# Matmuls without a reader in front of eleven waits of TensorE

## The chip, the cores and the metric

The kernel runs on one core of one Trainium2 chip. The metric is the device time of one execution in microseconds; each kernel is run several times and the median is given. TensorE, which does the matrix products, runs at one of two clock levels, 1.2 or 2.4 GHz. The trace shows which one it was granted, as a share of the full clock: 0.50 or 1.00.

## The reference

One call computes two blocks of two layers each, on 512 tokens of width 1024. The first block also carries 256 context tokens, the second one 16 meta tokens. Cut to what matters:

```python
for l in range(2):                                   # first block
    h  = modulate(rmsnorm(x, g_norm1[l]), sh1, sc1)
    hc = modulate(rmsnorm(xc, g_norm1[l]), sh1c, sc1c)
    pf, mq, mk, mv, mo, mg, cq, ckv, kr = split_proj(h @ w_in[l])   # and the same of hc
    y_f = fourier_mix(pf)
    y_m = mlstm_output(hf, hb, mo, g_mlstm[l])       # chunkwise scans in both directions
    y_a = merge_heads(blocked_attend(qn, qr, (lat_keys, ctx_keys)))
    x = x + ga1 * (jnp.concatenate([y_f, y_m, y_a], axis=-1) @ w_out[l])
    x = x + ga2 * sqrelu_mlp(modulate(rmsnorm(x, g_norm2[l]), sh2, sc2), w_up[l], w_down[l])
    ...                                              # the context likewise where l is 0
for i in range(2):                                   # second block
    h = hybrid_layer(h, attn_norm[i], w_in[i], ...)  # rmsnorm, fox attention, retention, gated MLP
out = rmsnorm_2(h, final_norm)[:, N_META:]
```

An rmsnorm needs the sum of the squares of all 1024 features of a token before the first feature can be scaled. Those sums stand at the edges between the stages.

## The kernel before

Activations lie with the features on the 128 partitions (8 tiles of 128 features, `KT`) and the tokens along the free dimension: 768 (`ALL`), 512 (`LAT`) or 528 (`SEQ2`). Weights come from memory in blocks of 128x1024. Each block is split into a high and a low part of reduced precision (`hi_ring` by ScalarE, L260; `lo_ring` by VectorE, L270), activations too (`h_hi`, `h_lo`), and each product is made three times: high by high, low by high, high by low (`tile_product`, L343). `product_pair` works on two weight blocks at once, the second three feature tiles behind the first (`LAG`), since it follows the operand tiles as they are made.

What the change touches:

- `Norm.on_pe` (line 677 on): the first norm of a layer. A product of `ones` and the sums of squares (`sumsq`, added up by GpSimd in L658) spreads the total over all partitions (`product`, L332). ScalarE takes the root (L690), VectorE inverts it (L706) and makes the operand tiles (L723, L716). In the first layer of the first block the squares are `presummed` in the stage before.
- `LateNorm.on_pe` (line 925 on): the norm in front of the first block's MLP, whose products start before the factor is known.
- the Fourier stage (line 1147 on), whose first product takes the tiles of `Norm`.
- the end of the mLSTM scans (line 2045 on): after the last chunk the outputs are normed and gated by the other engines, and TensorE turns them (transposes, L2050).
- `square_columns` in the mixing stage of the second block (line 2464 on): the sums of squares as columns (L2470 to L2477), and the products behind the first pair of weight blocks (line 2629 on), which wait until VectorE has taken a result out of PSUM (L2980).

Of the kernel before, what the change touches and what calls it, by code (L numbers as in the profile page):

```python
# [31 lines left out]
ALL = LAT + CTX  # L32
# [104 lines left out]
class Core:  # L137
# [68 lines left out]
    def buf(self, j):  # L206

        j %= BUFS
        return self.ps[:, 2 * j:2 * j + 2, :].rearrange("p b n -> p (b n)")

    def width(self, g):
        return NARROW if any(a <= g < b for a, b in self.narrow) else BLOCK
# [452 lines left out]
class Norm:  # L665
# [11 lines left out]
    def on_pe(self, pe):  # L677
        core = self.core
        if self.presummed:
            return  # L680
        pe.wait_ge(core.added.sem, core.added.at(0))
        product(core.nc, self.acc, [core.ones[:]], [core.sumsq[:]], self.tokens, P).then_inc(self.summed.sem, 1)

# [202 lines left out]
class LateNorm:  # L886
# [37 lines left out]

    def on_pe(self, pe):
        core = self.core
        pe.wait_ge(core.added.sem, core.added.at(0))
        product(core.nc, self.acc, [core.ones[:]], [core.sumsq[:]], self.tokens, P).then_inc(self.summed.sem, 1)

# [184 lines left out]
def fourier(core, arena, acts, mix, tokens, norm, l, mod_first, mods):  # L1114

    nc, dram = core.nc, core.dram
    tiles_of = [(0, LT, 0, LAT)] + ([(LT, TT, LAT, ALL)] if tokens == ALL else [])
    a = Alloc(arena, KT * ALL)
    u, spec = a(2, ALL), a(TT, 4 * P)
    half = [LAT // 2 + 1, CTX // 2 + 1] if not mods else [LAT, CTX]  # L1120
    at = [0, half[0]]
    cos = [a(LT, half[0]), a(CT, half[1])]
    sin = [a(LT, half[0]), a(CT, half[1])]

    mod = Modulation(core, l, mod_first, mods, a(MOD_RING, BLOCK).rearrange("p r n -> p (r n)"),
                     silu_rows(mix))
    norm.tmp = a(2, ALL)
    odd = u[:, :, 0:ALL]
    odd_in = core.counter("fourier_odd_copied")
    tables = core.counter("tables_in")  # L1130
    evacuated = core.counter("fourier_evacuated")
    feature = core.counter("fourier_features")
    token = core.counter("fourier_tokens")
    nt = tokens // P
    with nc.Block(no_gpsimd_drain=True) as block:
        @block.sync
        def _(sp):
            core.feed(sp, FOURIER_BLOCKS)
            if mods:
                mod.feed(sp)  # L1140

        @block.gpsimd
        def _(pool):
            for name, dst in (("cos_lat", cos[0]), ("sin_lat", sin[0]), ("cos_ctx", cos[1]), ("sin_ctx", sin[1])):
                pool.dma_start(dst, dram[name][:, :, 0:dst.shape[2]]).then_inc(tables.sem, 16)

        @block.tensor
        def _(pe):
            norm.on_pe(pe)

            product_pair(core, pe, 0, 0, UNROLL, KT, acts, tokens,
                         lambda j: pe.wait_ge(core.free.sem, core.free.at(j + 1)), norm.wait_tile(pe))
            pe.wait_ge(core.free.sem, core.free.at(BUFS + FOURIER_BLOCKS))
            for t in range(nt):
                if t >= 2:
                    pe.wait_ge(evacuated.sem, evacuated.at(t - 1))
                for j in range(2):
                    last = nc.tensor.matmul(core.ps[:, 4 + t % 2, j * 2 * P:(j + 1) * 2 * P],
                                            u[:, j, t * P:(t + 1) * P], core.const[:, C_DFT:C_END],
                                            start=True, stop=True)  # L1160
                last.then_inc(feature.sem, 1)
            pe.wait_ge(evacuated.sem, evacuated.at(nt))
            pe.wait_ge(tables.sem, tables.at(64))
            for j in range(2):
                for n, (t0, t1, c0, c1) in enumerate(tiles_of):
                    if mods:
                        for t in range(t0, t1):
                            for part, table in enumerate((cos[n], sin[n])):
                                last = nc.tensor.matmul(core.buf(j)[:, c0:c1],
                                                        spec[:, t, (2 * j + part) * P:(2 * j + part + 1) * P],  # L1170
                                                        table[:, t - t0, :], start=t == t0 and part == 0,
                                                        stop=t == t1 - 1 and part == 1)
                        continue
                    for part, table in enumerate((cos[n], sin[n])):
                        for t in range(t0, t1):
                            last = nc.tensor.matmul(core.ps[:, 2 * j + part, at[n]:at[n] + half[n]],
                                                    spec[:, t, (2 * j + part) * P:(2 * j + part + 1) * P],
                                                    table[:, t - t0, :], start=t == t0, stop=t == t1 - 1)
                last.then_inc(token.sem, 1)

        @block.scalar
        def _(act):
            mod.load_rows(act)
            norm.on_act(act)
            if mods:
                mod.sigmoid(act)
            for j in range(FOURIER_BLOCKS):
                core.part_hi(act, 0, j + SPLIT)
                core.computed(act, 0, j)
                nc.scalar.activation(u[:, j, 0:tokens], core.buf(j)[:, 0:tokens], ACT.Copy).then_inc(core.free.sem, 1)  # L1190
            if not mods:
                mod.sigmoid(act)
            for j in range(2):
                act.wait_ge(token.sem, token.at(j + 1))
                if mods:
                    nc.scalar.activation(mix[:, j, 0:tokens], core.buf(j)[:, 0:tokens], ACT.Copy)
                    continue
                n = at[len(tiles_of) - 1] + half[len(tiles_of) - 1]
                nc.scalar.activation(odd[:, j, 0:n], core.ps[:, 2 * j + 1, 0:n], ACT.Copy).then_inc(odd_in.sem, 1)

        @block.vector
        def _(dve):
            norm.on_dve(dve, norm.tmp)
            if mods:
                mod.begin(dve)
            for j in range(FOURIER_BLOCKS):
                core.part_lo(dve, 0, j + SPLIT)
            for t in range(nt):
                dve.wait_ge(feature.sem, feature.at(t + 1))
                nc.vector.tensor_copy(spec[:, t, :], core.ps[:, 4 + t % 2, :]).then_inc(evacuated.sem, 1)  # L1210
            if not mods:
                mod.begin(dve)
            if mods:
                mod.all_sums(dve)
                mod.finish(dve)
            for j in range(0 if mods else 2):
                dve.wait_ge(odd_in.sem, odd_in.at(j + 1))
                for n, (t0, t1, c0, c1) in enumerate(tiles_of):
                    h, e, o = half[n], core.ps[:, 2 * j, at[n]:at[n] + half[n]], odd[:, j, at[n]:at[n] + half[n]]
                    nc.vector.tensor_tensor(mix[:, j, c0:c0 + h], e, o, ALU.add)  # L1220
                    nc.vector.tensor_tensor(mix[:, j, c0 + h:c1][:, ::-1], e[:, 1:h - 1], o[:, 1:h - 1], ALU.subtract)
    core.close(FOURIER_BLOCKS, FOURIER_BLOCKS)
    mod.close()
    norm.close()
    tables.close(64)
    evacuated.close(nt)
    feature.close(nt)
    token.close(2)
    odd_in.close(0 if mods else 2)
# [662 lines left out]
def mlstm(core, arena, scratch, masks, pick, m, mix, ctx_out):  # L1892
# [8 lines left out]
    out = a(TT, hid)  # L1901
# [45 lines left out]
    with nc.Block(no_gpsimd_drain=True) as block:  # L1947
# [31 lines left out]
        def _(pe):  # L1979
# [57 lines left out]
            for u in range(len(steps_all)):  # L2037
                n = n_out(u)
                if u in outs and n + 1 < len(outs):
                    weigh(outs[n + 1])  # L2040
                if u in outs:
                    sums(u)
                if u in upds:
                    grow(u)
            for n, t in enumerate(tiles_done):
                pe.wait_ge(normed.sem, normed.at(n + 1))
                if n >= 4:
# [225 lines left out]
NORM_AT = 4  # L2273
# [12 lines left out]
def hybrid_layer(core, h, l):  # L2286
# [5 lines left out]
    entry, last = l == 0, l == DEPTH - 1  # L2292
# [133 lines left out]
    with nc.Block(no_gpsimd_drain=True) as block:  # L2426
# [34 lines left out]
        def _(pe):  # L2461
            free = lambda j: pe.wait_ge(core.free.sem, core.free.at(j + 1))

            def square_columns():

                pe.wait_ge(core.added.sem, core.added.at(0))
                if entry:
                    pe.wait_ge(gain_added.sem, gain_added.at(0))
                for t, (c, n) in enumerate(TOKEN_TILES[0:LT] if entry else TOKEN_TILES):
                    ins = nc.tensor.matmul(core.ps[0:n, NORM_AT, t:t + 1], core.sumsq[:, c:c + n], core.ones[:, 0:1],  # L2470
                                           start=True, stop=True)
                if entry:
                    for t in range(LT):
# [4 lines left out]
                                           start=True, stop=True)  # L2478
# [148 lines left out]
                    factor_rows()  # L2627
            ins.then_inc(core.done, 1)
            pe.wait_ge(ones_in.sem, ones_in.at(1))
            for j in range(2, MIX_BLOCKS):  # L2630
                w = core.arrived(pe, 0, j)
                free(j)
# [863 lines left out]
```

## Time and profile before

| | |
|---|---|
| median of three runs | 3328.93 us (3321.52, 3328.93, 3332.76) |
| profiled execution, first to last instruction (span) | 3326.5 us |
| TensorE, matmuls busy | 3110.3 us (94%), 19072 records |
| TensorE, weight loads busy | 2726.2 us (82%) |
| VectorE busy | 1787.3 us (54%) |
| ScalarE busy | 1176.6 us (35%) |
| GpSimd busy | 299.1 us (9%) |
| mean granted TensorE clock | 0.966 |

The profiled execution has no time of its own beside its span; the median of the runs lies 2.4 us above the span. Busy shares are over the whole span. Matmuls overlap in the pipeline, so the busy time of TensorE does not tell how fast it works; the granted clock does.

### The profile page before, as it was taken

To read this page: it belongs to the slowest core of one execution; us is meant where nothing else is said; L and a number is where in the kernel's file an instruction comes from. 1 tells how busy PE (TensorE), PEld (TensorE's weight loads), DVE (VectorE), ACT (ScalarE), POOL (GpSimd) and SP (SyncE) were. 2 spreads that over 40 slices of the span, in tenths; PEclk is the share of its full clock that TensorE was granted. 3 is DMA by queue.
4 is the path that set the end of the run, shared out by engine and by line. 5 is a ranking of instruction groups with operands and counts; after the bars stand their busy time and mean duration, and the time that the engine had idled before them with its cause. 6 is when DMAs were issued, how large, how long until landed. Compare 5 with 4: busy or idle time off the path is not lost. (4 is left out here: it accounts for less than half of the span.)

```text
span 3326.5 us, 49141 instructions
## 1 busy us (share of the span) xinstructions
PE 3110.3 (94%) x19072; PEld 2726.2 (82%) x19072; DVE 1787.3 (54%) x2840; ACT 1176.6 (35%) x1843; POOL 299.1 (9%) x268
## 2 busy tenths in 40 slices
PE   3999889999997999899999999999999999899998
PEld 2678877888886687789987897899999898778886
DVE  8558677465565567554443545554344345554444
ACT  3243534232232443544444332343223332243222
POOL 1000210101102001112223000010001000010001
PEclk8999889999998998899999999999999999999999
DMA  7231033232332231122222111122323211122322
GB/s 265 74 111 60 12 114 121 95 126 101 107 116 95 68 116 45 46 84 93 93 90 89 57 46 45 52 89 83 107 84 101 71 45 51 51 93 84 107 88 95
DMA packets 105693, 288.68 MB, mean 87 GB/s; under 512 B 36272, under 2 KB 36400, under 8 KB 104272
## 3 DMA queue, kind: packets, MB, share of 16 engines
q1 hardware_dynamic: 100304, 269.73, 24.3%
q0 software_dynamic: 3808, 10.38, 0.9%
q10 hardware_dynamic: 1440, 6.62, 0.5%
q8 instruction: 97, 1.59, 0.2%
q14 instruction: 44, 0.36, 0.0%
HBM read 284.56 MB, written 2.10 MB: 86 GB/s over the span
## 5 line engine op out<-in xcount | busy, mean ns | idle before, releaser
L343 PE MATMUL ps<-h_hi,hi_ring 128*128 128x512 f32 (+2 forms) x2672 | 872.3, 326 | 64.5 <-DVE h_lo L716 41.3
L270 DVE TENSOR_TENSOR lo_ring<-ring,hi_ring 128x1024 fp32r<-128x1024 f32 (+1 forms) x410 | 484.6, 1182 | 700.9 <-ACT hi_ring L260 696.6
L343 PE MATMUL ps<-h_lo,hi_ring 128*128 128x512 f32 (+2 forms) x2672 | 843.5, 316 | 0.0
L343 PE MATMUL ps<-h_hi,lo_ring 128*128 128x512 f32 (+2 forms) x2672 | 840.5, 315 | 0.0
L260 ACT ACTIVATE hi_ring<-ring 128x1024 fp32r<-128x1024 f32 (+1 forms) x410 | 420.1, 1025 | 1032.2 <-PE ps L343 992.0
L343 PEld LDWEIGHTS ps<-h_hi,hi_ring 128*128 128x128 f32 x2672 | 513.9, 192 | 126.5 <-issue 81.8
L343 PEld LDWEIGHTS ps<-h_lo,hi_ring 128*128 128x128 f32 x2672 | 515.1, 193 | 33.6 <-issue 3.9
L343 PEld LDWEIGHTS ps<-h_hi,lo_ring 128*128 128x128 f32 x2672 | 512.5, 192 | 30.9
L343 PE MATMUL ps<-ffn_operand,hi_ring 128*128 128x264 f32 (+1 forms) x2112 | 479.7, 322 | 1.5 <-DVE lo_ring L270 1.5
L343 PEld LDWEIGHTS ps<-ffn_operand,hi_ring 128*128 128x128 f32 x2112 | 350.5, 188 | 35.1 <-issue 1.8
L343 PE MATMUL ps<-ffn_operand,lo_ring 128*128 128x264 f32 (+1 forms) x1056 | 339.1, 321 | 0.0
L343 PE MATMUL ps<-hid_hi,hi_ring 128*128 128x512 f32 (+1 forms) x768 | 275.4, 359 | 3.3 <-DVE hid_lo L1087 3.3
L343 PE MATMUL ps<-hid_lo,hi_ring 128*128 128x512 f32 (+1 forms) x768 | 274.8, 358 | 0.0
L343 PE MATMUL ps<-hid_hi,lo_ring 128*128 128x512 f32 (+1 forms) x768 | 274.7, 358 | 0.0
L343 PE MATMUL ps<-hidden,hi_ring 128*128 128x264 f32 (+1 forms) x1056 | 239.4, 321 | 0.0
L343 PEld LDWEIGHTS ps<-ffn_operand,lo_ring 128*128 128x128 f32 x1056 | 198.4, 188 | 16.2
L343 PEld LDWEIGHTS ps<-hidden,hi_ring 128*128 128x128 f32 x1056 | 175.2, 188 | 16.3
L343 PE MATMUL ps<-hidden,lo_ring 128*128 128x264 f32 (+1 forms) x528 | 169.5, 321 | 0.0
L343 PEld LDWEIGHTS ps<-hid_hi,hi_ring 128*128 128x128 f32 x768 | 144.8, 189 | 28.4 <-DVE hid_lo L1087 5.1
L343 PEld LDWEIGHTS ps<-hid_hi,lo_ring 128*128 128x128 f32 x768 | 144.8, 189 | 23.1
L343 PEld LDWEIGHTS ps<-hid_lo,hi_ring 128*128 128x128 f32 x768 | 144.7, 188 | 22.8
L453 DVE SCALAR_TENSOR_TENSOR silu_rows<-mod_ring,silu_rows 128x1024 f32<-128x1024 f32 x128 | 150.1, 1218 | 1.2 <-DMA mod_ring<-w_mod_dram 1.2
(360 smaller groups left out, 3842.6 us busy)
## 6 DMA issues: line engine op xcount, KB each, us to landing
ring<-weights_dram SPq DMA_DIRECT2D x334, 512.0 KB, 3.3
mod_ring<-w_mod_dram SPq DMA_DIRECT2D x64, 512.0 KB, 4.2
ring<-weights_dram SPq DMA_DIRECT2D x76, 384.0 KB, 3.0
arena<-w_mod_dram SPq DMA_DIRECT2D x48, 512.0 KB, 3.4
x<-x_dram SPq DMA_DIRECT2D x1, 3072.0 KB, 16.6
arena<-c_rows_dram ACTq DMA_DIRECT2D x3, 1024.0 KB, 6.6
arena<-ret_decay_dram POOLq DMA_DIRECT2D x2, 1056.0 KB, 6.0
silu_rows<-c_rows_dram ACTq DMA_DIRECT2D x2, 1024.0 KB, 5.3
```

The source lines that it names most:

```text
L260: self.nc.scalar.activation(self.hi_ring[:, g % SPLIT, 0:w], self.ring[:, g % RING, 0:w], ACT.Copy).then_inc(self.hi, 1)
L270: self.nc.vector.tensor_tensor(self.lo_ring[:, g % SPLIT, 0:w], self.ring[:, g % RING, 0:w], self.hi_ring[:, g % SPLIT, 0:w], ALU.subtract ...
L343: ins = nc.tensor.matmul(out[0:m, c:c + n], w, a[:, t0:t0 + n], start=first and k == 0 and p == 0, stop=last and k == kts - 1 and p == 2)
L453: core.nc.vector.scalar_tensor_tensor(self.scratch[:, c, :], self.ring[:, g % MOD_RING, :], 1.0, self.rows[:, c, :], ALU.mult, ALU.mult, a ...
```

## The change

`Core.unread(n)` issues n matmuls of `ones` by `ones`, 128x128 in f32, into a corner of PSUM that nobody reads. They are called at the places named above, each time just ahead of a wait, with counts of 18 to 38.

```diff
--- before.py
+++ after.py
@@ -208,6 +208,13 @@
         j %= BUFS
         return self.ps[:, 2 * j:2 * j + 2, :].rearrange("p b n -> p (b n)")
 
+    def unread(self, n, out=None):
+
+        out = self.ps[:, 7, 384:512] if out is None else out
+        for _ in range(n):
+            self.nc.tensor.matmul(out, self.ones[:], self.ones[:, 0:out.shape[1]], start=True, stop=True,
+                                  skip_group_check=True)
+
     def width(self, g):
         return NARROW if any(a <= g < b for a, b in self.narrow) else BLOCK
 
@@ -678,6 +685,7 @@
         core = self.core
         if self.presummed:
             return
+        core.unread(24)
         pe.wait_ge(core.added.sem, core.added.at(0))
         product(core.nc, self.acc, [core.ones[:]], [core.sumsq[:]], self.tokens, P).then_inc(self.summed.sem, 1)
 
@@ -924,6 +932,7 @@
 
     def on_pe(self, pe):
         core = self.core
+        core.unread(24 if self.tokens == ALL else 19)
         pe.wait_ge(core.added.sem, core.added.at(0))
         product(core.nc, self.acc, [core.ones[:]], [core.sumsq[:]], self.tokens, P).then_inc(self.summed.sem, 1)
 
@@ -1147,6 +1156,11 @@
         @block.tensor
         def _(pe):
             norm.on_pe(pe)
+            if norm.presummed:
+                pe.wait_ge(norm.root.sem, norm.root.at(1))
+                core.unread(22)
+            else:
+                core.unread(38)
 
             product_pair(core, pe, 0, 0, UNROLL, KT, acts, tokens,
                          lambda j: pe.wait_ge(core.free.sem, core.free.at(j + 1)), norm.wait_tile(pe))
@@ -2042,6 +2056,7 @@
                     sums(u)
                 if u in upds:
                     grow(u)
+            core.unread(29, core.ps[:, 3, 384:512])
             for n, t in enumerate(tiles_done):
                 pe.wait_ge(normed.sem, normed.at(n + 1))
                 if n >= 4:
@@ -2463,6 +2478,7 @@
 
             def square_columns():
 
+                core.unread(26 if entry else 19)
                 pe.wait_ge(core.added.sem, core.added.at(0))
                 if entry:
                     pe.wait_ge(gain_added.sem, gain_added.at(0))
@@ -2627,6 +2643,7 @@
                     factor_rows()
             ins.then_inc(core.done, 1)
             pe.wait_ge(ones_in.sem, ones_in.at(1))
+            core.unread(18, core.ps[:, NORM_AT, 384:512])
             for j in range(2, MIX_BLOCKS):
                 w = core.arrived(pe, 0, j)
                 free(j)
```

The places in the order of the program. TensorE at the edge between the first layer's output projection and its MLP; `squares_added` is GpSimd's semaphore for the sums. Before:

```order
1638 L343 MATMUL ps<-h_hi,lo_ring 128x256
1639 L810 UNCONDITIONAL_BRANCH
1640 L1030 UNCONDITIONAL_BRANCH [waits barrier_Pool_Activation_PE_DVE_SP_release]
1641 L332 MATMUL ps<-sumsq,ones 128x512 [waits squares_added]
1642 L332 MATMUL ps<-sumsq,ones 128x256
```

The same place with the change (its lines stand 7 to 9 lower in the file):

```order
1641 L350 MATMUL ps<-h_hi,lo_ring 128x256
1642 L818 UNCONDITIONAL_BRANCH
1643 L1039 UNCONDITIONAL_BRANCH [waits barrier_Pool_Activation_PE_DVE_SP_release]
1644 L215 MATMUL ps<-ones 128x128 x24
1645 L339 MATMUL ps<-sumsq,ones 128x512 [waits squares_added]
1646 L339 MATMUL ps<-sumsq,ones 128x256
```

The 24 matmuls stand between the wait for the barrier and the product that waits for the sums; at four more edges it looks the same with other counts. TensorE behind the first pair of weight blocks of the mixing stage, where `psum_free` is VectorE's semaphore for a free buffer and `fox_ones_in` one for a constant row; with the change:

```order
4266 L350 MATMUL ps<-h_hi,lo_ring 128x264
4267 L215 MATMUL ps<-ones 128x128 [waits fox_ones_in]
4268 L215 MATMUL ps<-ones 128x128 x17
4269 L350 MATMUL ps<-h_hi,hi_ring 128x264 [waits psum_free,block_lo]
4270 L350 MATMUL ps<-h_lo,hi_ring 128x264
```

Here no barrier is in between: the 18 follow the last product of the pair, and the wait for the constant row has moved from the next product to them.

## Rows read from the trace of the kernel before

**Rows 1.** The page, 40 slices of the span: granted clock in tenths

```profile
PEclk8999889999998998899999999999999999999999
```

**Rows 2.** Who TensorE waited for: us in total, times, longest us

```profile
PE ps L343 <- DVE h_lo L716: 41.3, 6, 28.9
PE ps L332 <- POOL sumsq L658: 22.0, 4, 6.3
...
PE ps L343 <- DVE arena L2980: 9.5, 2, 4.8
...
PE ps L343 <- DVE h_lo L857: 5.6, 2, 3.2
```

**Rows 3.** Windows: stretch, length, TensorE busy (records), clock, DMA share, GB/s

```profile
505.42:508.40 2.98, 2.98 (x5) 0.50 0.98 403
1057.05:1059.98 2.93, 2.93 (x4) 0.50 0.95 377
1425.56:1430.00 4.44, 4.44 (x14) 0.50 0.83 229
1803.10:1812.30 9.20, 9.20 (x43) 0.50 0.73 270
...
sum 25.24, PE 25.23; mean PE 5.05
```

**Rows 4.** Windows behind other long waits

```profile
63.55:68.10 4.55, 4.55 (x13) 0.51 1.01 403
428.81:433.30 4.49, 4.49 (x14) 0.50 0.99 413
1373.28:1378.80 5.52, 5.52 (x13) 0.50 0.51 180
1834.47:1839.60 5.13, 5.13 (x23) 0.50 0.28 99
2602.63:2607.60 4.97, 4.97 (x23) 0.50 0.52 176
2607.60:2612.57 4.97, 4.97 (x43) 1.00 0.07 26
1069.57:1081.80 12.23, 10.42 (x22) 0.50 0.00 0
```

**Rows 5.** Barrier events of TensorE: duration ns, first and last start us

```profile
L810 PEldq EVENT_SEMAPHORE  x2: 51/51/51, 499.3 to 503.7; - x2
...
L1007 PEldq EVENT_SEMAPHORE  x2: 51/51/51, 1050.8 to 1055.4; - x2
...
L810 PEldq EVENT_SEMAPHORE  x2: 51/51/51, 1420.5 to 1424.4; - x2
...
L1007 PEldq EVENT_SEMAPHORE  x2: 51/51/51, 1796.6 to 1801.2; - x2
...
L2426 PEldq EVENT_SEMAPHORE  x2: 51/51/51, 2569.8 to 2573.7; - x2
```

**Rows 6.** Timeline at two edges: start us, us, what, [idle before <-releaser]

```profile
503.56 1.80 POOL L658 TENSOR_TENSOR sumsq<-sumsq,arena 128x768 f32<-128x768 f32 x1 [6.52 <-ACT arena L640]
...
505.42 2.93 PE L332 MATMUL ps<-sumsq,ones 128*128 128x512 f32 x4 [6.28 <-POOL sumsq L658]
...
2574.61 2.02 PE L2470 MATMUL ps<-ones,sumsq 128*128 128x1 f32 x10 [4.92 <-POOL sumsq L658]
```

**Rows 7.** Timeline of TensorE: transposes at the slow and at the full clock

```profile
420.99 0.90 PE L2050 MATMUL ps<-const,scratch 128*128 128x128 f32 x3 [7.55 <-ACT scratch L2121]
...
172.67 0.87 PE L1380 MATMUL ps<-const,arena 128*128 128x128 f32 x6 [0.79 <-ACT arena L1460]
```

**Rows 8.** Timeline around the first products of both Fourier stages

```profile
54.93 4.95 DVE L706 RECIPROCAL sumsq<-sumsq 128x768 f32<-128x768 f32 x1 [3.20 <-ACT sumsq L690]
...
1069.57 0.77 PE L343 MATMUL ps<-h_hi,hi_ring 128*128 128x512 f32 x1 [9.59 <-DVE h_lo L716]
...
1071.72 0.80 PE L343 MATMUL ps<-h_hi,hi_ring 128*128 128x512 f32 x1 [0.53 <-DVE h_lo L716]
```

## The prediction

> **What bounds the kernel now.** I read the slices of the page first: TensorE's granted clock is 8 to 9 tenths in most slices, not full [rows 1]. So some of its work runs at 1.2 GHz instead of 2.4 GHz. Next I read the list of waits, to see where the long pauses are: TensorE waits for `h_lo` of the norms, for GpSimd's last addition of squares, and for `arena L2980` [rows 2]. Then the windows from the end of each such wait to the point where the clock is back: the five in [rows 3] are 25.24 us together, all of them with TensorE busy and the clock at 0.50, and [rows 4] has six more (the fifth window there is what the same work looks like once the clock is back). Everything outside is product after product, so TensorE sets the end and a delay of it at a stage edge is carried to the last instruction.
>
> The price of a slow microsecond: 4.97 us at 0.50 hold 23 products, the next 4.97 us at 1.00 hold 43 [rows 4]. So of work that now runs slowly, a share of 1-23/43 = 0.47 would be saved. When the clock comes back: after a restart it takes 3.0 us (505.42 to 508.40), 4.4 (1425.56 to 1430.00) [rows 3], 4.6, 4.5, 5.1 and 5.0 (63.55, 428.81, 1834.47, 2602.63) [rows 4]. I take 4.5 us; the ends are 3.0 and 5.5 (1373.28 to 1378.80).
>
> **The change, part by part.** It removes and moves nothing. It adds 266 matmuls of 128x128 in f32 at eleven places, with no result that anyone reads. Their price has two bounds. Two f32 products in the code are four records in the trace (x4 at 505.42, [rows 6]), so one unread matmul is two records. A 128x128 record costs 0.21 us at the slow clock (three of `L2050` in 0.90 us, of which I count some 0.27 for the emptying of the pipeline) and 0.11 us at the fast one (six of `L1380` in 0.87 us, less some 0.2 of the same) [rows 7]. So an unread matmul costs 0.43 us cold and 0.22 us warm.
>
> *Five stage edges (24, 24, 19, 26, 19).* The waits there are 6.28 us before 505.42 and 4.92 us before 2574.61 [rows 6], and 24 warm unread matmuls are 5.3 us, so they seem to fit. But they stand behind the block's barrier, not at the start of the wait: the order shows the barrier's release on TensorE's queue, then the unread matmuls. The trace dates that release: TensorE's second event at the barrier is at 503.7, 1055.4, 1424.4, 1801.2 and 2573.7 [rows 5]. The actual wait ends at 505.42, 1057.05, 1425.56, 1803.10 [rows 3] and 2574.61 [rows 6]. So only 1.7, 1.6, 1.1, 1.9 and 0.9 us are left to hide in, 7.2 in all (7.0 with 0.05 us at each for the first instruction), because GpSimd's last addition starts at 503.56 and takes 1.80 us [rows 6], and the barrier opens just behind its start. And the clock has fallen by then: TensorE has been idle for four to five microseconds since the last product. So they start cold: 4.5 us until the clock is back hold 4.5/0.43 = 10.5 of them, the rest cost 0.22 each. 24 take 4.5+13.5x0.22 = 7.5 us, 19 take 6.4, 26 take 7.9; together 7.5+7.5+6.4+7.9+6.4 = 35.7. Less the 7.0 that is hidden: the next real product starts 28.7 us later in sum. Queued behind them is the product of the squares, for which ScalarE's root waits, and all products of the stage. What is given back: the 25.24 us of cold work run warm, 0.47x25.24 = 11.9 us. Net +16.8 us. Bounds: with 3.0 us until the clock is back the five take 31.8 us, so +12.9; with 5.5 us +19.3.
>
> At the fourth edge `h_lo` tiles come from ScalarE and VectorE behind the same column sums, so warm TensorE will catch up with them; I take 0.6 us back from the gain there (an estimate between 0 and the 1.5 us of one pair of products).
>
> *After the first pair of the mixing stages (18 and 18).* No barrier is in front: the order puts them right behind the pair, and the semaphore they wait for (`fox_ones_in`) was raised early. The clock is full when they start. They take 18x0.22 = 4.0 us in a wait of 4.75 us (9.5 us for two, [rows 2]). So they cost nothing and the clock should hold. 5.13+4.97 us of cold work [rows 4] become warm: -4.7 us. If the clock fell in the last 0.7 us anyway, this term would be 0.
>
> *At the end of the mLSTM scan (29 and 29).* The wait for the first tile is 7.55 us [rows 7], there is no barrier before it, but the clock is already down when it starts. 4.5+18.5x0.22 = 8.6 us: 1.0 us too late for the first transposes. The transposes themselves get shorter (6x3 at half the price, paced by ScalarE's copies of about half a microsecond), I count -0.5 us for both places, bounds +1 and -1.5. After them a barrier and the splitting of the mix leave TensorE idle again (3.24 us at the first place, [rows 2]), perhaps long enough for the clock to fall again: after 4.75 us it had, at 1834.47 [rows 2, 4]. So of the 4.49+5.52 us of cold work behind [rows 4], worth 4.7 us, I count half: -2.4 us, bounds 0 and -4.7.
>
> Here the Trainium skill has a rule that speaks against this part ("TensorE: Matmul & The Clock Gate", Part 4: PE-mode transpose): transposes do not engage the full clock. The six records of `L1380` are transposes and run at 0.11 us each [rows 7], at the full clock, so the trace does not bear it out for a stretch between other products. By the rule my 0.5 us for the shorter transposes would be gone and the sum half a microsecond longer.
>
> *First Fourier stage (22, behind the root) and the second one (38, behind the squares).* The root is in at 54.93 [rows 8]; the wait ends at 63.55. 4.5+11.5x0.22 = 7.0 us in 8.6 us: hidden. The 38 take 8.4 us in 9.59 us [rows 8]: hidden. But neither gains: the first tiles of `h_lo` come 2.15 us apart (1069.57 and 1071.72, [rows 8]), and TensorE, cold as it is, waits for 1.81 of the 12.23 us [rows 4]. Made faster, it only waits more, and being idle half the time it may lose the clock again when the pairs begin. I count +0.3 us for both, bounds -0.6 and +1.3.
>
> The sum, against the profiled execution: 28.7-11.9+0.6-4.7-0.5-2.4+0.3 = +10.1 us on a span of 3326.5 us, 3336.6 us. The median of the runs shown, 3328.93, lies 2.4 us above that span, so the forecast is 3339.0 us.
>
> **The rivals.**
> *Fitting covers (faster).* If the unread matmuls began when the wait begins (499.14, which is 505.42 less the 6.28 us of [rows 6]), all would be hidden and each cold restart warm: 0.47x(25.24+5.13+4.97+4.49+5.52) = 21.3 us, with the transposes 21.8 us: 3307 us. For it: the counts are about 0.85 of each wait at 0.22 us. Against it: the barrier's release in [rows 5] and the order. It decides at one place: whether the first unread matmul runs before 503.7.
> *Even (no change).* The clock comes back after 3.0 us, as at 505.42, and holds after the scans: late 31.8-7.0 = 24.8, less 11.9, 4.7 and 4.7+0.5, is +3 us: 3332 us. For it: one row of six. Against it: the other five.
> *The unread work doesn't raise the clock.* Then each costs 0.43 us: 48.2-7.0 = 41.2 at the edges, 9.8 at the scans (12.5 against 7.55, twice), 6.7 at the 38, 6.0 at the two 18s, 0.9 at the first: about +65 us, 3394 us. Against it: f32 products of the same kind precede the rise at 505.42 [rows 6].
>
> **How the numbers follow.** The forecast has 0.6, the even case 0.22, the fitting covers 0.08, no rise 0.04; the other 0.06 is for small gains of mechanisms that I don't see. A measurement tells about 0.3% (10 us) from no change, and the forecast of +10.1 lies on that edge: a little over half of it counts as slower, since three of the six restarts of a plain product took 4.6 us or more. That is 0.33, with the 0.04 of no rise and 0.1 of the even case, where the runs fall high by chance: slower 0.47. Same is the rest of the forecast and of the even case and 0.02 of the small gains, 0.41. Faster is 0.08 and the other 0.04 of these, 0.12. The forecast's own range is 3332 to 3346 us; the stated one is 3328 to 3348, leaving out the fitting covers and the case of no rise.
>
> **What would show it.** The unread matmuls start at about 503.8, never at 499.2, and in records 0.21 us apart at first; the product of squares starts some 6 us behind GpSimd's end at the five edges, with TensorE never idle there; the clock's windows behind it read 1.00. At the mixing stages the product after the 4.75 us wait starts at full clock. The second Fourier stage has the same length as before from `h_lo` on. I am wrong if an edge from barrier to product is under 4 us, if the clock falls in the 0.7 us left behind the 18s, or if the time stays under 3329 us.

## The result, and the profile after

The changed kernel takes 3342.11 us in the median (3339.42 to 3345.95, six runs) against 3330.76 us before (3321.52 to 3334.40, six runs). The ratio is 1.0037 with a 95% interval of 1.0024 to 1.0049: slower by 11.4 us, which is small but clear of no change. The forecast was 3339.0 us. In the page of the profiled execution TensorE's clock is up and so is the time:

```profile
span 3340.9 us, 50205 instructions
...
PE 3166.2 (95%) x19604; PEld 2784.5 (83%) x19604; DVE 1788.0 (54%) x2840; ACT 1177.1 (35%) x1843; POOL 299.1 (9%) x268
...
PEclk8999899999999998999999999999999999899999
```

The 532 additional records are the 266 unread matmuls, two each. The mean granted clock rose from 0.966 to 0.975. So the change did what it says, and the kernel still lost: a busier TensorE and a fuller clock are not a shorter path.

TensorE's two events at each barrier, to be compared with [rows 5] (duration ns, first and last start us):

```profile
L818 PEldq EVENT_SEMAPHORE  x2: 51/51/51, 500.1 to 504.6; - x2
...
L1016 PEldq EVENT_SEMAPHORE  x2: 51/51/51, 1054.8 to 1059.4; - x2
...
L818 PEldq EVENT_SEMAPHORE  x2: 51/51/51, 1429.8 to 1433.7; - x2
...
L1016 PEldq EVENT_SEMAPHORE  x2: 51/51/51, 1808.6 to 1813.3; - x2
...
L2441 PEldq EVENT_SEMAPHORE  x2: 51/51/51, 2581.3 to 2585.2; - x2
```

And the timeline at the five edges (start us, length us; in brackets the idle time before and what ended it), the answer to [rows 6]:

```profile
504.39 1.81 POOL L665 TENSOR_TENSOR sumsq<-sumsq,arena 128x768 f32<-128x768 f32 x1 [6.51 <-ACT arena L647]
...
504.67 7.93 PE L215 MATMUL ps<-ones 128*128 128x128 f32 x48 [4.70 <-PEq L818]
512.45 1.02 PE L339 MATMUL ps<-sumsq,ones 128*128 128x512 f32 x2
...
1059.16 1.81 POOL L665 TENSOR_TENSOR sumsq<-sumsq,sq 128x768 f32<-128x768 f32 x1 [6.63 <-ACT sq L647]
...
1059.52 7.04 PE L215 MATMUL ps<-ones 128*128 128x128 f32 x48 [4.85 <-PEq L1016]
1066.39 1.46 PE L339 MATMUL ps<-sumsq,ones 128*128 128x512 f32 x4
...
1433.49 1.27 POOL L665 TENSOR_TENSOR sumsq<-sumsq,arena 128x512 f32<-128x512 f32 x1 [4.14 <-ACT arena L647]
...
1433.78 6.11 PE L215 MATMUL ps<-ones 128*128 128x128 f32 x38 [4.10 <-PEq L818]
1439.72 1.02 PE L339 MATMUL ps<-sumsq,ones 128*128 128x512 f32 x2
...
1813.38 7.67 PE L215 MATMUL ps<-ones 128*128 128x128 f32 x52 [4.85 <-PEq L1016]
1813.63 1.40 POOL L665 TENSOR_TENSOR x<-x,sq_gain 128x512 f32<-128x512 f32 x1
1820.88 0.95 PE L2486 MATMUL ps<-ones,sumsq 128*128 128x1 f32 x8
...
2584.24 1.81 POOL L665 TENSOR_TENSOR sumsq<-sumsq,arena 128x528 f32<-128x528 f32 x1 [6.66 <-ACT arena L647]
...
2585.29 5.91 PE L215 MATMUL ps<-ones 128*128 128x128 f32 x38 [4.12 <-PEq L2441]
2591.04 1.08 PE L2486 MATMUL ps<-ones,sumsq 128*128 128x1 f32 x10
```

What to see: the idle time before the unread matmuls is 4.70, 4.85, 4.10, 4.85 and 4.12 us and ends with `PEq`, the barrier, not with GpSimd. GpSimd's last addition ends at 506.20, 1060.97, 1434.76, 1815.03 and 2586.05; the product of squares starts at 512.45, 1066.39, 1439.72, 1820.88 and 2591.04. Before, it started 0.05 to 0.15 us behind that addition. It is 6.2, 5.4, 4.9, 5.7 and 4.9 us late, 27.1 us together.

The clock in the windows from the first unread matmul on (stretch, length, TensorE busy and records, clock, DMA share, GB/s):

```profile
504.67:509.60 4.93, 4.93 (x23) 0.50 0.81 294
509.60:512.45 2.85, 2.85 (x28) 1.00 0.56 227
512.45:517.00 4.55, 4.55 (x25) 1.00 0.00 0
1059.52:1062.50 2.98, 2.98 (x14) 0.50 0.60 203
...
1433.78:1434.60 0.82, 0.82 (x7) 1.00 0.00 0
1434.60:1438.01 3.41, 3.41 (x18) 0.50 0.76 153
...
1813.38:1816.88 3.50, 3.50 (x17) 0.51 0.69 227
...
2585.29:2588.30 3.01, 3.01 (x14) 0.50 0.63 196
...
1849.24:1854.37 5.13, 5.13 (x42) 1.00 0.32 97
2616.42:2621.40 4.98, 4.98 (x41) 1.00 0.52 166
429.34:434.50 5.16, 5.15 (x15) 0.50 1.00 408
...
1383.70:1386.80 3.10, 3.10 (x7) 0.50 0.88 325
...
1079.58:1084.00 4.42, 3.30 (x6) 0.50 0.00 0
```

At the first edge the unread matmuls run cold (at the slow clock) for 4.9 us (23 records, 0.21 us each) and warm (at the full clock) after it. From one start to the next a warm record takes 0.11 us; the 28 of the second window include records that reach over its edges. The products of the stage then start at 1.00. At the second, fourth and fifth edge the cold part is 3.0, 3.5 and 3.0 us. At the third the group starts at the full clock, after 4.10 us of idle time; the clock falls only 0.8 us later and is back after 3.4 us. The two starts of the mixing stages (1849.24, 2616.42) hold 42 and 41 products at 1.00 in the length in which there were 23 at 0.50 [rows 4]. The output projections behind the scans (429.34, 1383.70) are cold again, the first for 5.2 us (4.5 before, [rows 4]), the second for 3.1 us (5.5 before). In the second Fourier stage the clock falls again while the first tiles come (1079.58), after pauses of only 1.10 and 1.22 us:

```profile
1077.43 0.47 PE L350 MATMUL ps<-h_hi,hi_ring 128*128 128x512 f32 x1 [1.10 <-DVE h_lo L724]
...
1079.58 0.80 PE L350 MATMUL ps<-h_hi,hi_ring 128*128 128x512 f32 x1 [1.22 <-DVE h_lo L724]
```

VectorE issues the same 2840 instructions in both kernels, so each can be paired with itself. The difference of their start times, changed less before, tells where the 14.4 us between the two spans came from:

```
stretch (us of before)          change of the difference, us
edge at 505                      +3.6
edge at 1057                     +4.0
edge at 1425                     +2.8   (+3.85 at the product, -1.08 after it)
edge at 1803                     +2.7   (+4.04, -1.31)
edge at 2574                     +2.5   (+4.21, -1.70)
mixing stages, 1834 and 2602     -2.3 and -2.25
ends of the scans, 421 and 1368  -0.6 and -1.9
Fourier stages, 63 and 1069       0.0 and 0.0
all the rest                     +5.9   (of it +1.2 at 240, +3.3 at 1334 to 1338, +1.4 at 2908)
```

### The profile page after: what moved, and what is told of

Its sections match the earlier page's. It is cut to its first block and busy times, and to the rows that moved or that the text cites. A ratio compares the mean times of both kernels' runs of the same rounds, so it can differ in the third digit from the quotient of the medians.

```text
span 3340.9 us, 50205 instructions
## 1 busy us (share of the span) xinstructions
PE 3166.2 (95%) x19604; PEld 2784.5 (83%) x19604; DVE 1788.0 (54%) x2840; ACT 1177.1 (35%) x1843; POOL 299.1 (9%) x268
```

## The experiments

The time of before, run beside each group, was 3328.52 us (25 runs, first four kernels) and 3329.53 us (17 runs, next four).

### Only the five edges

```diff
-            if norm.presummed:
-                pe.wait_ge(norm.root.sem, norm.root.at(1))
-                core.unread(22)
-            else:
-                core.unread(38)
...
-            core.unread(29, core.ps[:, 3, 384:512])
...
-            core.unread(18, core.ps[:, NORM_AT, 384:512])
```

> Only the five unread groups behind the barriers of the stage edges (24, 24, 19, 26, 19); the six others are taken out. Theory (they start cold behind the barrier and run past the end of the wait; cold work behind them is given back): the edges alone cost 2.5 to 4.0 us each, +15.6 us together by the shifts between the two traces, so about 3346 us against 3330.8, more than the full change. Rival (the edges are neutral, the loss comes from the six others or from clock falls elsewhere): 3331 us, no change.

Measured: 3345.42 us (3343.17 to 3347.02), ratio 1.0052 (1.0039 to 1.0065). So 16.9 us slower than before, as the theory said, and the rival that the edges are neutral is out.

### Only the six others

```diff
-        core.unread(24)
...
-        core.unread(24 if self.tokens == ALL else 19)
...
-                core.unread(26 if entry else 19)
```

> Only the six other groups (22, 29, 38, 29, 18, 18), none behind a barrier. Theory: -4.6 us at the two mixing stages and -2.5 us at the ends of the two scans, nothing at the Fourier stages: about 3324 us against 3330.8. Rival (the loss of the full change comes from these): 3335 us or more. Rival (warm restarts are worth nothing, the clock falls again anyway): 3331 us.

Measured: 3325.82 us (3317.57 to 3327.61), ratio 0.9986 (0.9977 to 0.9996): faster by 4.7 us by the ratio, by 2.7 us by the medians. Four of the twelve runs lie at 3317.6 to 3318.4 us, the others at 3322.7 to 3327.6, and the trace is from one of the four. The rival that the loss comes from these groups is out. Of the 7.1 us that were expected, the middle of the interval has two thirds. The two halves of the change add up: by the ratios 0.52% less 0.14% is 0.38%, against the 0.37% of the whole.

### The edges' matmuls ahead of the barrier

The edges' own groups are taken out. Others stand at the end of TensorE's list in the block before, in this order in the cuts: the output projection, the first block's MLP (behind its loop) and the layer of the second block.

```diff
+            core.unread(18 if tokens == ALL else 15)
...
+                core.unread(18 if mods else 18)
...
+            core.unread(15 if l + 1 < DEPTH else 0)
```

> The five groups of the stage edges stand at the end of the block before, ahead of the barrier, with 18, 18, 15, 18 and 15 matmuls, so that at 0.22 us each they end before the barrier opens; the six others as in the change. Theory: nothing is late; after the barrier 1 to 2 us of idle time are left, so the clock should still be full when the product of squares starts; of the 25.24 us of cold work at the edges 11.9 us are saved, with the 7.1 us of the others -19 us: about 3312 us. If the remaining pause lets the clock fall in half of the cases: 3318 us. Rival (the place does not matter, unread work costs what it takes): 84 matmuls of 0.22 us or more, 3340 us or more.

Measured: 3319.28 us (3314.83 to 3321.63), ratio 0.9973 (0.9962 to 0.9984), 9.2 us faster than before, not 19. The direction is right, the size of the main case is missed by half; the time is near the 3318 us that the expectation named for a clock that falls again in half of the pauses. The rival that the place does not matter is out. The timeline and the windows of its trace show why in part:

```profile
500.90 4.18 PE L215 MATMUL ps<-ones 128*128 128x128 f32 x36
505.49 1.81 POOL L665 TENSOR_TENSOR sumsq<-sumsq,arena 128x768 f32<-128x768 f32 x1 [6.52 <-ACT arena L647]
...
507.35 2.07 PE L339 MATMUL ps<-sumsq,ones 128*128 128x512 f32 x2 [2.26 <-POOL sumsq L665]
```

```profile
507.35:510.80 3.45, 3.45 (x6) 0.51 0.99 402
1804.40:1811.30 6.90, 6.90 (x34) 0.51 0.82 294
```

The 18 matmuls take 4.18 us from the end of the last product and nothing is late: the product starts 0.05 us behind GpSimd's end. But 2.26 us of idle time are left before it, and the clock fell at three of the five edges: here as the product starts, and 1.2 and 2.1 us into the work that follows the pauses of 2.63 and 1.58 us at the fourth and fifth (at 1804.4 and 2572.4). It held over 2.33 and 1.78 us at the two others. A further part of what is missing is that the six other groups, as measured above, bring 4.7 us and not 7.1.

### The edges' matmuls behind the barrier, cut to what the wait holds

```diff
-        core.unread(24)
+        core.unread(3)
...
-        core.unread(24 if self.tokens == ALL else 19)
+        core.unread(3 if self.tokens == ALL else 2)
...
-                core.unread(26 if entry else 19)
+                core.unread(4 if entry else 2)
```

> The five groups stay behind the barrier but have 3, 3, 2, 4 and 2 matmuls, so that at 0.43 us each they end before the wait does; the six others as in the change. Theory (the loss is the count that runs past the wait): nothing is late, and the clock comes back 1 to 2 us earlier at each edge, worth 0.47 of that, some 3 us in all, with the 7.1 us of the others: about 3321 us. Rival (any unread work behind the barrier costs, whatever its count, for example by the start of the instruction stream): 3330 us or more.

Measured: 3319.43 us (3314.99 to 3324.87), ratio 0.9973 (0.9964 to 0.9982), 9.1 us faster. In its trace the product of squares starts 0.05 to 0.22 us behind GpSimd's end, so nothing is late. At the same place with a count that fits there is no loss. That the place as such costs, whatever the count, is out: what made the change slow is what runs past the end of the wait.

### Both pieces

The groups ahead of the barriers as above, and shorter ones behind them.

```diff
+            core.unread(18 if tokens == ALL else 15)
...
-        core.unread(24)
+        core.unread(6)
...
+        core.unread(6 if self.tokens == ALL else 4)
...
+                core.unread(7 if entry else 3)
```

> The unread work of the stage edges in two pieces: 18, 18, 15, 18 and 15 matmuls ahead of the barrier, and 6, 6, 4, 7 and 3 behind it, sized to end before the wait does; the six others as in the change. With the first piece alone (3319.3 us) the clock still fell at three of the five edges in the pause of about 2.3 us that was left. Theory (that pause is what kept the gain small): the clock reads 1.00 over all five edges, about 4 us less, 3315 us. Rival (what is missing from the 19 us that were hoped for are clock falls in other stages, which no edge cures): the same 3319 us.

Measured: 3314.33 us (3311.94 to 3319.19), ratio 0.9957 (0.9944 to 0.9970), 15.2 us faster than before. The clock at all five edges, in windows around them:

```profile
499.00:512.00 13.00, 11.55 (x78) 1.00 0.43 161
1048.00:1062.00 14.00, 13.17 (x100) 1.00 0.38 143
1418.00:1432.00 14.00, 13.25 (x97) 1.00 0.29 82
1795.00:1808.00 13.00, 11.48 (x94) 1.00 0.54 185
2560.00:2575.00 15.00, 14.23 (x119) 1.00 0.54 191
```

It reads 1.00 throughout, so with the second group behind the barrier the clock does stay up over the edges. What that is worth against the moved version is not shown by the times: the medians are 5.0 us apart, as expected, but the two intervals overlap (0.9944 to 0.9970 and 0.9962 to 0.9984).

### Without the Fourier stages, with the output projections

The 22 and the 38 are left out, a group stands ahead of each output projection, and the 15 also follow the last layer.

```diff
-            if norm.presummed:
-                pe.wait_ge(norm.root.sem, norm.root.at(1))
-                core.unread(22)
-            else:
-                core.unread(38)
...
             if mix is not None:
+                core.unread(8 if tokens == ALL else 6)
                 product_pair(core, pe, 0, 0, UNROLL, KT, acts, tokens, free,
...
+            core.unread(15)
```

> As the two-piece version, without the 22 and 38 of the Fourier stages, with 8 and 6 more behind the barrier ahead of the output projections (a pause of 3.24 and 2.36 us in which the clock fell again after the scans), and 15 at the end of the last block. Theory: 22 and 38 are worth nothing, the output projections start at the full clock and save up to 0.47 of their 10.0 us of cold work: 2 to 4 us less than the two-piece version, about 3312 us. Rival (the clock after the scans is lost for other reasons, or the 38 do help the second Fourier stage): equal to it or above.

Measured: 3310.85 us (3305.76 to 3319.69), ratio 0.9954 (0.9937 to 0.9970). The lowest median of all, 18.7 us below before, but no run lies near it: three are at 3305.8 to 3306.8 us and three at 3314.9 to 3319.7. By the ratio it is 15 us faster, and its interval covers that of the two-piece version, so a further gain is not shown. Against the changed kernel both are clearly faster. What the edit was for did happen in its trace: the first output projection, cold from 429.34 on in the changed kernel, runs at the full clock.

```profile
425.00:436.00 11.00, 9.65 (x60) 1.00 0.74 271
```

### Only the Fourier stages

The five edges' groups, the 29s and the 18s are taken out, the 22 and the 38 stay.

> Only the 22 and the 38 of the two Fourier stages. Theory (their first tiles come at VectorE's pace, so that a faster TensorE only waits more): no change, 3328.5 us, within 3 us; at the first Fourier stage the clock may fall once more, +1 to +3 us. Rival (cold work behind them is saved like elsewhere, 0.47 of 12.23 and 4.55 us): 3320.6 us.

Measured: 3330.26 us (3325.28 to 3332.93), ratio 1.0000 (0.9991 to 1.0009). No change, and the rival of 3320.6 us is out. The windows over the first products of the two Fourier stages, and TensorE's timeline of the second with what it waited for:

```profile
59.95:70.19 10.24, 6.53 (x41) 1.00 1.02 414
70.19:73.60 3.41, 3.21 (x9) 0.50 0.14 54
1069.57:1090.00 20.43, 14.49 (x64) 1.00 0.00 0
```

```profile
1071.71 0.47 PE L350 MATMUL ps<-h_hi,hi_ring 128*128 128x512 f32 x1 [0.40 <-DVE h_lo L723]
1073.86 0.50 PE L350 MATMUL ps<-h_hi,hi_ring 128*128 128x512 f32 x1 [1.21 <-DVE h_lo L723]
1076.10 0.50 PE L350 MATMUL ps<-h_hi,hi_ring 128*128 128x512 f32 x1 [1.27 <-DVE h_lo L723]
```

The second stage is a stretch whose clock went from 0.50 to 1.00 and that gained nothing: the tiles still come 2.15 to 2.33 us apart, as in the kernel before, and the pauses grew from 0.53 us ([rows 8]) to 1.2 and more. In the first stage the clock was up for the first three tiles and then fell once more for 3.4 us (70.19), as the expectation feared.

### The edges' counts doubled

```diff
-        core.unread(24)
+        core.unread(48)
...
-        core.unread(24 if self.tokens == ALL else 19)
+        core.unread(48 if self.tokens == ALL else 38)
...
-                core.unread(26 if entry else 19)
+                core.unread(52 if entry else 38)
```

> The change with the counts of the five edges doubled (48, 48, 38, 52, 38). Theory (behind the barrier the count runs on the path, and what is added comes after the clock is back): 133 more matmuls at 0.22 us are 29 us more than the change, 3371 us. Rival (part of them is hidden in the wait): clearly less, 3355 us or below. If they ran at the slow clock: 3399 us.

Measured: 3360.98 us (two runs, 3359.09 and 3362.86), ratio 1.0097 (1.0079 to 1.0114): 18.9 us above the change's 3342.11, not 29. The 29 rest on a wrong count. The edges' groups have 24+24+19+26+19 = 112 matmuls, so doubling adds 112 and not 133; the page shows it too (19828 records against 19604, two for each). At 0.22 us they are 24.6 us, which gives about 3367 us. VectorE's pairs between the traces of the two kernels show +5.1, +5.5, +5.4, +5.7 and +4.0 us at the edges, 25.7 us for 112 matmuls or 0.23 us each. The first edge in its trace:

```profile
503.44 13.25 PE L215 MATMUL ps<-ones 128*128 128x128 f32 x96 [4.70 <-PEq L818]
...
516.53 1.46 PE L339 MATMUL ps<-sumsq,ones 128*128 128x512 f32 x4
```

So the whole dose lands on the path at the edges, at about the warm price; none of it is hidden. The spans of the two traces differ by 20.2 us, 5.5 less than the edges. Of these, 4.6 lie between 1300 and 1360 us of the changed kernel, in the second layer's scans, which neither kernel touches: there the clock was at 0.50 for 17.1 us in this trace (1330.87 to 1347.94) and for 27.3 us in that of the changed kernel. The next experiment shows how much that stretch varies by itself.

### Each kernel profiled once more

Before and changed kernel, no edit.

> The kernel before, unchanged, profiled once more. Theory (the granted clock falls and rises at other moments in each execution, so that stages that the change does not touch differ by some us between two traces): the stages from the first latent attention to the scans and the mixing stages differ by up to 1 to 3 us each from the first trace of the same kernel, with no instruction changed; the span between 3322 and 3334 us. Rival (the traces of one kernel agree and the 5.9 us of the change's trace outside its eleven places come from the change): every stage agrees with the first trace within 0.5 us.

> The changed kernel, profiled once more. Theory: the lateness of the five stage edges repeats (5 to 6 us each from the end of GpSimd's last addition to the product of squares), while the extra 3.3 us of the second layer's scans and the 1.2 us of the first latent attention don't, or turn up elsewhere. Rival: both repeat, and belong to the change.

Measured: spans of 3325.4 us and 3340.8 us. Between the two traces of the kernel before, VectorE's pairs move by +1.5 us between 75 and 100 us and by -3.3 us between 1300 and 1350, with no instruction changed. Between the two traces of the changed kernel the edges repeat: the product of squares is 6.2, 6.6, 4.9, 5.9 and 5.1 us late (6.2, 5.4, 4.9, 5.7 and 4.9 in the first). The +1.2 at 240 does not repeat, and of the +3.3 at 1334 to 1338 about half does: from 1300 to 1350 the second trace has +1.7 against the first of before.

That stretch can be read. The low clock in it, in the two traces of the kernel before and then in the first of the changed kernel:

```profile
1310.51:1331.00 20.49, 14.82 (x75) 0.50 0.00 0
...
1312.87:1323.11 10.24, 7.23 (x37) 0.50 0.00 0
...
1318.54:1345.85 27.31, 21.64 (x107) 0.50 0.00 1
```

The second trace of the changed kernel has 23.9 us of it. Over all twelve traces the stretch from 1300 to 1350 of before is 46.6 to 46.7 us long where 10.2 us are cold, 50.0 where 20.5 are and 53.2 where 27.3 are, and the others lie in the same order. So the difference there is time at the low clock, and two executions of one kernel differ in it by 10 us. Whether the change makes it longer is not settled by two traces each: the kernels with the edges alone, the moved matmuls and both pieces have 23.9 us in their one trace, the one with the Fourier stages alone 20.5, and those with the six others alone, with the cut counts and with the output projections 10.2.

## Why the prediction was right

**The bound and the price of the cold clock.** Right. The mixing stages went from 23 to 42 and 41 products in the same time. Two readings were loose. The window that shows the same work at the full clock (2607.60) is the sixth of [rows 4], not the fifth. And the bounds of 3.0 to 5.5 us for the clock's return leave out the 9.20 us at 1803.10 in [rows 3], where products of one column come first.

**Five edges.** Right in mechanism, size a little high. The release of the barrier was read off [rows 5], and all five groups started about 0.1 us behind it. Predicted lateness 28.7 us, measured 27.1. I had taken 4.5 us cold for all; it was 4.9 us at the first edge and 3.0 to 3.5 at the four others. The groups so took 33.8 us and not 35.7, and 6.7 us of that were hidden and not 7.0. That all of them start cold was wrong at the third edge, where the clock fell only 0.8 us after the start. Net of what is given back 15.6 us by the pairs of instructions, against 16.8+0.6 predicted. The kernel with the edges alone (+16.9 us), the one with cut counts (no loss) and the doubled one (+25.7 us at the edges for 112 more matmuls) show that it is the count past the end of the wait.

**Mixing stages.** Right: -4.7 us predicted, -4.55 measured. The idle time left was 1.24 us and not 0.7, and it did not drop the clock (1849.24).

**Ends of the scans.** Right within the bounds, the halving by luck: -2.9 us predicted, -2.5 measured, unevenly. The groups of 29 took 7.9 and 7.6 us, not 8.6, since the clock was back 3.0 and 2.0 us after their start; so the transposes were hardly late. Behind both scans the clock had fallen again when the projection began. At the first it came back no earlier than before, and only the 0.6 us of the transposes were won; at the second it came back 2.4 us earlier.

**Fourier stages.** Right: nothing gained, shown by the kernel with these alone. The reason was VectorE's pace, as said. The fear that the clock would be lost again is borne out at both stages in the changed kernel's trace (65.85 and 1079.58), and at the first one in that of the Fourier stages alone (70.19); there it held over the second. It cost nothing that the time shows.

**Rivals.** Fitting covers: out, by the start at 504.67. No rise: out, by the rise at 509.60. Even: out by the interval of the result. Its condition at the edges nearly held, though (3.0 to 3.5 us at four of the five), so this rival deserved more than "one row of six"; its other condition, a full clock behind the scans, did not.

**What I did not have.** The sum over the eleven places is 8.5 us in the traces (15.6-4.55-2.5), the difference of the spans 14.4 us, the difference of the medians 11.4 us. About 3 to 6 us lie in stretches that the change does not touch, 3.3 us of it in the one stretch of the scans read above. The forecast of +10.1 came within 1.3 us of the median's difference in part by luck: the two errors, an edge term 1.8 us too high and nothing for the rest, had opposite signs.

## What to carry to other kernels

Filler work in front of a wait is free only from the moment the queue can start it: look for the barrier or semaphore that it stands behind, and size it by the time from that release to the wait's end, at the clock that is granted at that moment. Here the waits of 4.9 to 6.7 us had 0.9 to 1.9 us behind the barrier; 264 matmuls of the same kind instead of 266, those of the edges part ahead of the barrier and part behind it, turned +11 us into -15 us. And filler pays only where the engine sets the pace of what follows: behind the Fourier norms the clock doubled and the time stayed.

## What the runs showed of the hardware

- How long a pause the clock outlasts was not one number here. It was down after 2.26 us of idle time at one edge of the moved version (507.35) and held over 2.33 us at another; it was down after 3.24 us at 429.35. After 4.10 us at the third edge it was still up and fell 0.8 us into the next work. Within one stage it held over repeated pauses of 1.2 to 1.4 us between short products (1.00 from 1069.57 to 1090.00 in the kernel with the Fourier stages alone), and fell in the same stage of the changed kernel after pauses of 1.10 and 1.22 us (1079.58).
- Unread matmuls of ones by ones raise it as products on data do: it rose 4.9 us after their start at 504.67 and 2.0 to 3.5 us after their start, or after the fall, at the other four edges and the scans.
- Two traces of the same kernel differ by up to 3.3 us in a stage of short turns, by 10 us more or less at the low clock. A change of 3 us can't be read from one trace of each kernel.
